# A hybrid attention layer on one core: the first weight quarter issued by ScalarE ahead of the load of g

## The reference

```
h = rmsnorm(x, norm_pre_g)                  # g below: 1024 factors, one per column
u = h @ w_in                                # 1024 x 4096, eight groups of 512 columns
A = differential attention, 4 heads         # two softmax maps, second one scaled by lambda
B = block-sparse (MoBA) attention, 8 heads  # past blocks of 256 plus the own causal block
y = concat(A * silu(gate_A), B * silu(gate_B)) @ w_out
out = x + rmsnorm(y, norm_post_g)
```

## Time and profile before

| | |
|---|---|
| median of 3 runs | 254.14 us (254.02 to 254.44) |
| the profiled execution | 254.23 us |
| its span, first to last instruction | 252.4 us |
| TensorE busy | 245.6 us (97%) |
| VectorE, ScalarE, GpSimd busy | 177.0, 143.0, 32.7 us |
| HBM read and written | 29.04 and 2.13 MB |

### The profile page before, as it was taken

One profiled execution on the slowest core, in us unless ns is written; L12 is line 12 of the kernel. 1 busy time (PEld: TensorE's weight loads), 2 busy tenths in 40 slices (PEclk: granted clock), 3 DMA queues, 4 the chain that ended last, 5 costly groups with the idle time before them and its releaser, 6 DMA issues.

```text
span 252.4 us, 4450 instructions
## 1 busy us (share of the span) xinstructions
PE 245.6 (97%) x1567; PEld 123.2 (49%) x1567; DVE 177.0 (70%) x393; ACT 143.0 (57%) x336; POOL 32.7 (13%) x74
## 2 busy tenths in 40 slices
PE   8999999999999999999999999999999999999991
PEld 6454444445444554544455444454444444555570
DVE  2998585587478688868877767977787896835313
ACT  4777565375356666574677595667565665611110
POOL 1329300000000320041031033000000000111101
PEclk9999999999999999999999999999999999999998
DMA  6978979605656545544935644568849869982422
GB/s 242 366 245 173 310 251 371 218 28 135 106 160 163 180 114 130 140 163 112 203 103 136 137 161 119 136 189 184 174 103 201 209 157 170 202 203 43 125 86 83
DMA packets 59674, 42.47 MB, mean 168 GB/s; under 512 B 45808, under 2 KB 46072, under 8 KB 59652
## 3 DMA queue, kind: packets, MB, share of 16 engines
q1 hardware_dynamic: 59636, 42.18, 63.5%
q10 hardware_dynamic: 16, 0.00, 0.0%
HBM read 29.04 MB, written 2.13 MB: 123 GB/s over the span
## 4 chain that ended last, share of the span: by engine, by line
PE 97%; DVE 1%; DVEq 0%; POOLq 0%; issue 0%; ACT 0%; POOL 0%; ACTq 0%
PE unit_ps L578 72%; PE score_ps L634 6%; PE o_ps L655 5%; PE unit_ps L608 4%; PE unit_ps L589 3%; PE unit_ps L615 2%; PE unit_ps L543 1%; PE score_ps L536 1%; PE score_ps L709 1%; PE unit_ps L709 1%; DVE area L1058 0%; DVE gates L956 0%; DVEq L180 0%; POOLq L180 0%; ACT junk L732 0%
## 5 line engine op out<-in xcount | busy, mean ns | idle before, releaser
L578 PE MATMUL unit_ps<-area,w_hi 128*128 128x512 f16 x256 | 76.2, 379 | 0.0
L788 ACT ACTIVATE arena<-arena,negmax 128x512 f32<-128x512 f32 (+3 forms) x64 | 35.4, 554 | 49.5 <-DVE negmax L985 49.4
L578 PE MATMUL unit_ps<-w_hi,area 128*128 128x512 f16 x192 | 60.3, 379 | 0.0
L578 PE MATMUL unit_ps<-area,w_lo 128*128 128x512 f16 x128 | 48.5, 379 | 0.0
L578 PEld LDWEIGHTS unit_ps<-area,w_hi 128*128 128x128 f16 x256 | 24.1, 98 | 27.2 <-issue 1.1
L578 PE MATMUL unit_ps<-w_lo,area 128*128 128x512 f16 x96 | 36.4, 379 | 0.0
L985 DVE CUSTOM_DVE_ANT_0 arena<-score_ps,strips 128x512 f32<-128x512 f32 (+3 forms) x64 | 28.6, 485 | 9.2 <-PE score_ps L634 9.2
L882 DVE SCALAR_TENSOR_TENSOR w_lo<-stage,g_cols,w_hi 128x512 f16<-128x512 f32 x32 | 24.2, 755 | 11.3 <-ACT w_hi L746 11.2
L578 PEld LDWEIGHTS unit_ps<-w_hi,area 128*128 128x128 f16 x192 | 18.8, 98 | 21.9 <-DVE w_lo L888 0.7
L745 ACT ACTIVATE w_hi<-stage,g_cols 128x512 f16<-128x512 f32 x32 | 22.7, 711 | 7.3 <-DMA stage<-in_w_in_dram 7.3
L884 DVE SCALAR_TENSOR_TENSOR w_lo<-stage,g_cols,w_hi 128x512 f16<-128x512 f32 x32 | 24.8, 777 | 0.0
(11 more groups left out here) (106 smaller groups left out, 357.7 us busy)
## 6 DMA issues: line engine op xcount, KB each, us to landing
stage<-in_w_in_dram SPq DMA_DIRECT2D x32, 512.0 KB, 4.3
stage<-in_w_out_dram SPq DMA_DIRECT2D x8, 512.0 KB, 4.2
arena<-in_x_dram SPq DMA_DIRECT2D x4, 512.0 KB, 5.2
strips<-bias_rows SPq DMA_DIRECT2D x4, 512.0 KB, 4.7
stage<-in_x_dram SPq DMA_DIRECT2D x4, 512.0 KB, 4.7
out_dram<-area SPq DMA_DIRECT2D x3, 512.0 KB, 2.7
strips<-bias_rows SPq DMA_DIRECT2D x1, 1024.0 KB, 7.8
pt<-arena SPq DMA_TRANSPOSE x32, 3.1
```

The lines of the kernel that those rows point to most:

```text
L578: last = nc.tensor.matmul(bank, a, b, start=(k == 0 and n == 0), stop=(k == KT - 1 and n == 2))
L788: nc.scalar.activation(probs[:, i % 2, m, 0:n], probs[:, i % 2, m, 0:n], ACT.Exp, bias=negmax[:, i, m:m + 1], scale=-1.0, accum_out=sums[: ...
```

## The change

Quarter 0 is no longer issued by SyncE behind x[0]. ScalarE issues it as its first instruction, and issues the load of g after it. SyncE issues quarter 1 directly behind x[0]. The destination, the semaphore and the sizes are the same, and no wait is added or removed.

```diff
@@ SyncE
             load_x(0)
-            load_quarter(0)
             load_quarter(1)
             load_x(1)
@@ ScalarE
+            first = GROUPS[0][2]
+            nc.scalar.dma_start(stage[:, 0, :].rearrange("p (k n) -> p k n", k=2),
+                                w_in_v[:, 0:2, first:first + WIDTH]).then_inc(w_loaded[0], 16)
             nc.scalar.dma_start(g_rows[:, :], norm_pre_g[0].rearrange("(k p) -> k p", p=P)).then_inc(gpre_loaded, 16)
             x_square(0)
```

## The result

The changed kernel takes 257.0 us (median of 6 runs, 256.67 to 257.8) against 254.08 us before in the same comparison. The ratio is 1.0115, with a 95% interval of 1.0101 to 1.0129, so the change costs 2.9 us. The profiled execution has a span of 255.2 us, 2.8 more than before.

A forecast was written before the change was run, and what follows sets the result against it. TensorE was taken to bound the kernel, so the change is worth its shift of quarter 0's start: 2.5 late less 0.22 absorbed, 2.25 us on the profiled 254.23 us, or 256.4 us on the median's scale; range 255.1 to 257.8.

The forecast's parts named there:

- What bounds the start: Start of quarter 0's products: delays there delay the end; quarter 0 lands 0.63 us before it is used.
- x[0]'s share: DMA engines at the start: x[0] divides them with quarter 0 and lands at 5.08 instead of 4.43.
- the alternation: DMA engines take one row of each queue in turn: x[0] 4 KB, quarter 0 2 KB; x[0] needs 1.5 times 1.29 us.
- g's landing: Behind quarter 0 on ScalarE's queue, quarter 0's second half alternating with quarter 1: g lands at about 6.4.
- From g to quarter 0: TensorE and VectorE work between g's landing and quarter 0's products: 1.95 us at high clock, 2.93 at low.
- The clock: TensorE's pause before g may keep the lower clock until quarter 0: start 2.0 to 2.95 us late, middle 2.5.
- rival C: Clock stays low into quarter 0's products: 3.6 us late, 3.4 net, 257.5 us; chance 20%.
- What comes back: Before quarter 2, TensorE's hidden wait of 0.22 us absorbs delay; quarter 2 lands when it did.
- A: At the start, quarter 0 wins the DMA engines or both share bytes evenly: 254.8 to 255.2 us; chance 15%.
- B: x[0] wins the DMA engines, quarter 0 then alternates with quarter 1, g lands at 7.0: 256.5 to 257.5 us; 15%.
- Rival D: Not slower: g lands by 4.0, x[0] still at 4.43, TensorE gains 0.22 us before quarter 2; 253.9 us; 5%.

The follow-up runs named there:

- e5: The changed kernel with quarter 1 also issued by ScalarE, behind quarter 0 and ahead of the load of g; 260.01 us, ratio 1.0211.
- e8: e1 with SyncE holding back quarter 1 and x[1] until g has landed; 254.44 us, ratio 1.0000.
- e9: The kernel before with x[0] issued by ScalarE, g behind it, and quarter 0 first on SyncE's queue; single run, 257.63 us.
- e1: The changed kernel with ScalarE's two issues swapped, the load of g first and quarter 0 behind it; 257.84 us, ratio 1.0144.
- e6: The kernel before without TensorE's five first warm-up products; 255.17 us, ratio 1.0026.
- e2: The changed kernel with g issued by SyncE as its first instruction, ahead of x[0]; 257.12 us, ratio 1.0109.

## Why the prediction was right, and where it was off

The forecast was 256.4 us and the measured time is 257.0, inside the range. Point by point:

- *What bounds the start.* Right: the start of quarter 0's products is what counts, its landing had time to spare, in the changed kernel the start waits for g alone, and the delay reached the end but for 0.3 us (0.22 on record).
- *x[0]'s share.* 5.08 on record, 4.61 measured. From 3 to 4 us the two queues moved 59 and 75 packets, about even in rows, as the alternation has it. But from 2 to 3 us it was 65 to 3, so quarter 0 hardly ran while the first half of x[0] (0.27 of 0.52 MB) went through. The queues of the changed kernel (packets, MB, share of the engines) from 2 to 3 and then from 3 to 4 us:

```profile
q1 hardware_dynamic: 65, 0.27, 72.7%
q10 hardware_dynamic: 3, 0.01, 1.6%
...
q1 hardware_dynamic: 59, 0.21, 53.0%
q10 hardware_dynamic: 75, 0.15, 39.3%
```

- *g's landing.* 6.4 on record, 5.51 measured. The step that failed is that the second half of quarter 0 alternates with quarter 1. Quarter 1 was issued 0.44 us later, and it hardly ran while quarter 0 did: from 4 to 5 us the changed kernel moved 192 packets on ScalarE's queue and 30 on SyncE's. e5, e8 and e9 show the order of issue in its place; e1 shows its limit, two transfers issued 0.31 us apart that did share.
- *From g to quarter 0.* At the low clock 2.93 was on record, 3.02 measured (5.51 to 8.53). What stands behind the wait for g was priced right.
- *The clock.* I took the middle between high from the start and low until quarter 0. It was low for longer, into the products of quarter 0, which cost 0.93 more. That is the mechanism of rival C, which had 20%, and not of the forecast. C's own time was too long because it took g at 6.4; its price for the slow products, 1.6 of them at 0.43 more each, so 0.7, was below the 0.93. So the term of the sum read 2.5 - 0.22, and should have read 2.18 + 0.93 - 0.3. Two sizes were off: g by 0.9 us too late, and the clock by 1.5 too little (3.02 from g to quarter 0 where the middle had 2.45, and 0.93 behind it). The first hid more than half of the second, so that the time is nearer than its parts is luck. With g at its measured 5.51 and the rest as on record the forecast would have been 255.5.
- *What comes back.* On record quarter 2 "lands when it did"; it landed by 9.64 instead of 10.87. That changed nothing here, since TensorE came to it later still. e6, with its transfers issued as in the kernel before, had it by 9.89, so the change need not be the cause.
- *Rivals A and B.* Neither came: x[0] was not held for a whole transfer, and g did not wait for quarter 1. The page "DMA: Bandwidth & Descriptors" of the Trainium skill, section "Queues, rings and completion order", has a switch only after a whole packet of descriptors, from which the prediction concluded A or B. That was a wrong reading: B lets quarter 0 alternate with quarter 1, while whole packets, x[0] first, would land quarter 0 one transfer behind x[0], with g, by an estimate from the rows at about 5.7 (4.43 and 1.29), and x[0] at 4.61 with g at 5.51 is near that. Whether an engine switched by packet or by row the trace doesn't tell, since its rows don't name the engine. The page's other rule, in the section "Issuing engines are not separate DMA queues", that a second issuing engine saves issue time only, agrees with e8's ratio of 1.0000.
- *Rival D.* It asked for g by 4.0; g came at 5.51.

What stays open: why quarter 0, issued in the same moment as x[0], got 3 packets to 65 at first, in both arrangements of the engines (e9 has 24 to 53 from 2 to 3 us), and why x[1] and quarter 0 did share in e1. Issues 0.44 us and more apart were served in their order in the changed kernel and in e2 and e8; what decides between closer ones, and where the order is kept, no run shows.

## What to carry to other kernels

Issue a small load that everything waits for, here 4 KB of g, before the large ones on *any* queue: here each 512 KB issued earlier cost it 1.0 to 1.4 us (e5: 2.7 for two more, one on either queue; e9: 1.0 after x[0], for one on the other queue). Moving a transfer that has time to spare off one queue gains nothing if it puts a needed one behind it. Where a pause of TensorE at the start of a kernel is predicted, count the clock too: here the pause of 2.1 us cost some 1.6 us more in slow transposes and products, and five more dummy products brought 1.1 back in the span.

## What the runs showed of the hardware

- Transfers on SyncE's and ScalarE's queues were served about in the order of issue over both in the changed kernel, e2 and e8, where the issues of competing ones were 0.44 us or more apart: from 4 to 5 us the changed kernel moved 192 packets of ScalarE's queue (quarter 0, issued at 0.73) and 30 of SyncE's (mostly quarter 1, issued at 1.17). Held to a closer order it fails: in e1, where quarter 0 was issued at 1.34 between quarter 1 (1.17) and x[1] (1.65), it shared with x[1], and its landing moved from 5.72 to 8.45 us.
- Where two large transfers do share, the counts of rows can come out even, and not the bytes. In e1, from 6 to 7 us, x[1] with rows of 4 KB and quarter 0 with 2 KB pieces moved nearly the same count, and so twice the bytes for x[1] (packets, MB, share):

```profile
q1 hardware_dynamic: 67, 0.27, 66.6%
q10 hardware_dynamic: 66, 0.14, 34.6%
```

- TensorE's clock can be lost again early on: in e1 it was high when the transposes ended (a warm-up pair in 0.39 us), then TensorE waited 2.31 us for quarter 0, which it began at 8.59. The granted clock was 0.61 in the mean from 9 to 10 us and 0.50, the lower level, from 10 to 12.
- The moment of the rise was not fixed by the work: after the same work it came during the transposes of x[0] in the kernel before (1.30 us for eight) and behind them in e8 (1.77).
